# Moving a token mix to GpSimd and cutting three small products into narrow tiles, in a two-block transformer kernel on one core

## The reference, cut to what matters

```python
x_prev = jnp.pad(x, ((0, 0), (1, 0), (0, 0)))[:, :T]
xx = x_prev - x
xs = x[None] + xx[None] * mu[:, None, None, :]      # six mixes
r, k, v = (products of xs[0], xs[1], xs[2] with w_rkv)
w_log = -softplus(-(w0 + tanh(xw @ w1) @ w2)) - 0.5  # xw, xa, xg = xs[3], xs[4], xs[5]
a = sigmoid(a0 + (xa @ a1) @ a2)
g = sigmoid(xg @ g1) @ g2                            # g1 is 1024 x 160
kk = kk / max(sqrt(sum(kk * kk)), 1e-12)             # k * k_k, per head of 64
S, y = scan over the tokens
y = ((y - mean) * rsqrt(var + LNX_EPS)) * lnx_w + lnx_b   # per head of 64
out = ((y + bonus) * g) @ w_o
```

## Time and profile before

| | |
|---|---|
| Median of 3 executions | 1356.43 us (1354.27 to 1356.81) |
| The profiled execution: its time, its span | 1354.54 us, 1352.8 us |
| PE busy | 1318.0 us (97%) |
| DVE busy | 934.7 us (69%) |
| ACT busy | 654.6 us (48%) |
| POOL busy | 96.2 us (7%) |
| Granted TensorE clock, mean | 1.000 |

### The profile page before, as it was taken

The page is one execution under the profiler, slowest core; times in us unless marked ns, Lnnn a source line. Parts: engine busy times, 40 slices in busy tenths (PEclk is TensorE's granted clock), DMA queues, the critical chain, the costliest instruction groups (busy, mean ns, idle before and its releaser), DMA issues.

```text
span 1352.8 us, 23308 instructions
## 1 busy us (share of the span) xinstructions
PE 1318.0 (97%) x9276; PEld 1134.2 (84%) x9276; DVE 934.7 (69%) x1613; ACT 654.6 (48%) x977; POOL 96.2 (7%) x97
## 2 busy tenths in 40 slices
PE   7999999999999999999999998999999999999999
PEld 5987987888888988888888887888888888888887
DVE  6783356877777775877777588666666796576664
ACT  4431323644445775644444577543334568444441
POOL 0003153000000020000001000000001042000000
PEclk9999999999999999999999999999999999999999
DMA  8531213655553233665551550874531432573610
GB/s 241 215 125 64 66 65 99 226 190 192 192 163 110 70 125 112 219 196 189 186 186 62 187 187 1 311 296 171 202 125 63 165 113 75 205 285 138 243 62 32
DMA packets 111126, 208.10 MB, mean 154 GB/s; under 512 B 3872, under 2 KB 53408, under 8 KB 110528
## 3 DMA queue, kind: packets, MB, share of 16 engines
q1 hardware_dynamic: 111040, 206.88, 44.6%
HBM read 205.82 MB, written 1.05 MB: 153 GB/s over the span
## 4 chain that ended last, share of the span: by engine, by line
PE 85%; DVE 8%; ACT 5%; issue 1%; POOL 0%; DMA 0%; SPq 0%; DVEq 0%; ACTq 0%; POOLq 0%
PE ps L991 21%; PE ps L966 18%; PE ps L877 11%; PE ps L971 10%; PE ps L1060 2%; PE ps L1029 2%; PE ps L1377 2%; PE ps L1163 2%; PE ps L1284 1%; PE ps L942 1%; DVE Al L2514 1%; ACT Ah L1775 1%; PE ps L1420 1%; PE ps L1434 1%; ACT arena L2060 1%
## 5 line engine op out<-in xcount | busy, mean ns | idle before, releaser
L966 PE MATMUL ps<-hTx,Ah 128*128 128x512 f32 x1088 | 270.7, 391 | 0.0
L2521 DVE TENSOR_TENSOR Al<-ringA,Ah 128x2048 fp32r<-128x2048 f32 x76 | 173.8, 2287 | 103.4 <-ACT Ah L1785 103.4
L966 PEld LDWEIGHTS ps<-hTx,Ah 128*128 128x128 f32 x1088 | 199.8, 188 | 38.4
L971 PEld LDWEIGHTS ps<-hTx,Al 128*128 128x128 f32 x1152 | 156.7, 191 | 10.6
L971 PE MATMUL ps<-hTx,Al 128*128 128x256 f32 x1152 | 160.7, 283 | 0.0
L1820 ACT COPY xn<-ps 128x512 f32<-128x512 f32 x72 | 42.3, 587 | 243.6 <-PE ps L971 236.3
L1785 ACT CAST Ah<-ringA 128x2048 fp32r<-128x2048 f32 x76 | 145.8, 1919 | 16.7 <-PE ps L877 13.9
L1794 ACT CAST Bh<-ringB 128x1024 fp32r<-128x1024 f32 (+1 forms) x76 | 107.1, 1409 | 89.5 <-PE ps L991 89.5
L877 PE MATMUL ps<-Ah,hTx 128*128 128x512 f32 (+1 forms) x576 | 136.2, 387 | 1.1 <-ACT hTx L1765 0.9
L991 PE MATMUL ps<-Bh,hidh 128*128 128x512 f32 x432 | 135.0, 392 | 1.6 <-issue 1.1
L991 PE MATMUL ps<-Bl,hidh 128*128 128x512 f32 x432 | 134.3, 390 | 0.0
(11 more groups left out here) (433 smaller groups left out, 2013.4 us busy)
## 6 DMA issues: line engine op xcount, KB each, us to landing
ringA<-in_ffn_w_in SPq DMA_DIRECT2D x44, 1024.0 KB, 7.5
ringA<-in_mlp_w SPq DMA_DIRECT2D x32, 1024.0 KB, 7.5
ringB<-in_mlp_w SPq DMA_DIRECT2D x32, 1024.0 KB, 6.9
ringB<-in_ffn_w_out SPq DMA_DIRECT2D x44, 512.0 KB, 4.3
ringA<-in_diff_w_in SPq DMA_DIRECT2D x12, 1024.0 KB, 6.3
ringA<-in_dsa_w_in SPq DMA_DIRECT2D x8, 1024.0 KB, 6.4
ringA<-in_w_k SPq DMA_DIRECT2D x4, 1024.0 KB, 8.3
ringA<-in_w_r SPq DMA_DIRECT2D x4, 1024.0 KB, 7.2
```

Of the source, the lines that this page charges most:

```text
L966: mm(o.rearrange("p (i t) -> p i t", i=2), w_hi, hTx[:, :, k * T:(k + 1) * T], start=(k == 0), stop=False)
L971: last = mm(o[:, T:2 * T], Al[:, half, k * T + j * P:k * T + j * P + P], hTh[:, k, :], start=False, stop=(k == KT - 1))
L2521: V.tensor_tensor(a_split(w, Al, half), a_half(w, (a_at[w] + par) % 2, half), a_split(w, Ah, half).bitcast(F32), ALU.subtract).then_inc(al ...
```

## The change

Four edits, all in the first mixer:

1. **Mix 1 moves to GpSimd.** Per half, four `tensor_scalar` (`xx * mu`, 128x256) and one `tensor_tensor` (`+ hT`, 128x1024). It waits for `xx_rdy`, which VectorE's `shifted` raises, and raises `xa_rdy`.
2. **Narrow tiles.** The gate's last 32 columns are made chunk by chunk into four column tiles of 32 (32 matmuls of 64 columns for 8 of 256); `key_sums` likewise; `key_factors` becomes 32 products of 32 rows and 64 columns, and the root, clamp and inverse act on 64 columns for 256. The second gate product uses 32 rows at partitions 32c, so g2's last rows are loaded four times, with no clearing. Four dummy products (`keep(4, 7)`) are put behind the first gate product.
3. **Order of the gates.** `gates_wide((0, 1))` behind h1, `gates_narrow((0, 1))` behind h2, both pairs 2 and 3 behind the scan.
4. **Chunk 3's norm by lanes.** VectorE does mean, centring and squares for 256 columns at a time, lane 0 before lane 1; GpSimd scales lane 0 and adds its bonus, VectorE does so for lane 1.

```diff
-                             (g2b_sb[0:GLORA - P, :], d["a_g2"][P:GLORA, :]),
+                             *[(g2b_sb[32 * c:32 * c + 32, :], d["a_g2"][P:GLORA, :]) for c in range(NCK)],
...
                 for k in range(KT):
                     a0 = CON["sel"][0] + 14 - 2 * k
-                    last = mm(ps[:, 0, 0:T], con[:, a0:a0 + P], xnflat[:, k * T:(k + 1) * T],
-                              start=(k == 0), stop=(k == KT - 1))
+                    for j in range(4):
+                        o = k * T + j * CH
+                        last = mm(ps[32 * j:32 * j + 32, 0, 0:CH], con[:, a0:a0 + 32],
+                                  xnflat[:, o:o + CH], start=(k == 0), stop=(k == KT - 1))
...
-                for k in (0, 2, 4, 6, 1, 3, 5, 7):
-                    r = slice(32 * (k // 2), 32 * (k // 2) + 32)
-                    last = mm(ps[:, k // 2, (k % 2) * T:(k % 2) * T + T],
-                              spread[r, k * P:(k + 1) * P], kinv[r, :], start=True, stop=True)
+                for k in range(KT):
+                    for j in range(4):
+                        r = slice(32 * j, 32 * j + 32)
+                        last = mm(ps[:, j, k * CH:k * CH + CH], spread[r, k * P:(k + 1) * P],
+                                  kinv[r, :], start=True, stop=True)
...
+            for k in range(KT):
+                o = k * wl + 2 * LORA + P
+                for c in range(NCK):
+                    last = mm(ps[32 * c:32 * c + 32, b, T:T + CH], ringA[:, a % 2, o:o + 32],
+                              xi[:, k, c * CH:c * CH + CH], start=(k == 0), stop=(k == KT - 1))
             last.then_inc(job_rdy, 1)
+            keep(4, 7)
...
+            def gate_part(c, i, left, right, first):
+                return mm(ps[head_rows(i), c, :], left,
+                          right.rearrange("p (k i n) -> p k i n", k=KT, i=2)[:, :, i, :],
+                          start=first, stop=not first)
...
                 if (u, name) == (7, "h1"):
-                    gates(0)
+                    gates_wide((0, 1))
                 elif (u, name) == (7, "h2"):
-                    gates(1)
+                    gates_narrow((0, 1))
...
+            i, buf = MIXES[1]
+            for half in range(2):
+                pool.wait_ge(xx_rdy, half + 1)
+                ks = slice(4 * half, 4 * half + 4)
+                for k in range(4 * half, 4 * half + 4):
+                    last = G.tensor_scalar(fm(buf)[:, k, :], fm(xx)[:, k, :], col("mu", 8 * i + k), None,
+                                           ALU.mult)
+                link(last)
+                G.tensor_tensor(fm(buf)[:, ks, :], fm(buf)[:, ks, :], hT[:, ks, :], ALU.add
+                                ).then_inc(xa_rdy, 1)
...
+            pool.wait_ge(wk["rstd"], 4)
+            link(G.tensor_tensor(groups(y), groups(y), bc(g, 2, 64), ALU.mult))
+            link(G.tensor_tensor(y, y, row("lnx_w")[:, 0:256], ALU.mult))
+            G.tensor_tensor(y, y, bv3[:, 0:256], ALU.add).then_inc(wk["yn"], 1)
...
             shifted(0, 4)
             mix(0, 0)
-            mix(1, 0)
             dve.wait_ge(ha_rdy, 4)
             shifted(4, 8)
             mix(0, 1)
-            mix(1, 1)
...
+            for l in range(2):
+                y, d3, g, _r = last_lane(l)
+                dve.wait_ge(*EV_N[6 + l, "Y"])
+                link(V.tensor_reduce(g, groups(y), AX_X, ALU.add))
+                link(V.tensor_scalar(g, g, 1.0 / HD, None, ALU.mult))
+                link(V.tensor_tensor(groups(y), groups(y), bc(g, 2, 64), ALU.subtract))
+                link(V.tensor_tensor(d3, y, y, ALU.mult))
+                V.tensor_reduce(g, groups(d3), AX_X, ALU.add).then_inc(ss_rdy, 1)
```

More of the change, by code:

```diff
@@ L211, in program @@
         xs_rdy = sem("xs_rdy")
+        xa_rdy = sem("xa_rdy")
+        xx_rdy = sem("xx_rdy")
         wk = {n: sem("wk_" + n) for n in
@@ L1136, in _ @@
                     if k % 4 == 0:
[L1137 removed]
+                        pe.wait_ge((xs_rdy, xa_rdy)[i], k // 4 + 1)
                     o = k * wl + i * LORA
@@ L1143, in _ @@
             xi = fm(MIXES[2][1])
[L1144 to L1150, removed]
+            for k in range(KT):
+                if k % 4 == 0:
+                    pe.wait_ge(xs_rdy, 3 + k // 4)
+                o = k * wl + 2 * LORA
+                mm(ps[:, b, 0:T], ringA[:, a % 2, o:o + P], xi[:, k, :],
+                   start=(k == 0), stop=(k == KT - 1))
+            for k in range(KT):
+                o = k * wl + 2 * LORA + P
+                for c in range(NCK):
+                    last = mm(ps[32 * c:32 * c + 32, b, T:T + CH], ringA[:, a % 2, o:o + 32],
+                              xi[:, k, c * CH:c * CH + CH], start=(k == 0), stop=(k == KT - 1))
             last.then_inc(job_rdy, 1)
+            keep(4, 7)
             for s in range(4):
@@ L1208, in need, with gates_wide, gates_narrow @@
                 pe.wait_ge(*EV_N[u, name])
-            def gates(c):
-                for s, w in ((0, g2a_sb), (T, g2b_sb)):
-                    for i in range(2):
[L1214 to L1219, removed]
+            def gate_part(c, i, left, right, first):
+                return mm(ps[head_rows(i), c, :], left,
+                          right.rearrange("p (k i n) -> p k i n", k=KT, i=2)[:, :, i, :],
+                          start=first, stop=not first)
+            def gates_wide(cs):
+                for c in cs:
+                    for i in range(2):
+                        gate_part(c, i, sigg[:, c * CH:c * CH + CH], g2a_sb, True)
+            def gates_narrow(cs):
+                for i in range(2):
+                    for c in cs:
+                        r = slice(32 * c, 32 * c + 32)
+                        last = gate_part(c, i, sigg[r, T:T + CH], g2b_sb[r], False)
+                        if i:
+                            last.then_inc(wk["g"], 1)
             for u, name in ORDER:
@@ L1313, in _ @@
                 if (u, name) == (7, "h1"):
-                    gates(0)
+                    gates_wide((0, 1))
                 elif (u, name) == (7, "h2"):
-                    gates(1)
[L1318 to L1321, removed]
+                    gates_narrow((0, 1))
+            need(6, "Y")
+            gates_wide((2, 3))
+            gates_narrow((2, 3))
             need(7, "Y")
@@ L2004, in _ @@
                     gn_root(2)
-            gn_root(3)
+            for i, name in enumerate(("lnxc3a", "lnxc3b")):
+                root(name, gs_[:, 56 + 4 * i:60 + 4 * i], gs_[:, 24 + 4 * i:28 + 4 * i], HD, eps_l)
             act.wait_ge(wk["g"], NCK)
@@ L2305, in rest_slot @@
                                 ).then_inc(al_rdy, 1)
[L2307 to L2314, removed]
+            pool.wait_ge(cols_in, 16)
+            i, buf = MIXES[1]
[8 more added lines that the diff above has]
+                                ).then_inc(xa_rdy, 1)
             pool.wait_ge(con_in, 16)
@@ L2889, in _, with last_lane @@
                 gate(c)
[L2890 to L2899, removed]
-            for c in (2, 3):
-                gate(c)
+            def last_lane(l):
+                return (chunk(ytok, 3)[:, 256 * l:256 * l + 256], dl[:, 256 * l:256 * l + 256],
+                        gs_[:, 24 + 4 * l:28 + 4 * l], gs_[:, 56 + 4 * l:60 + 4 * l])
+            for l in range(2):
[6 more added lines that the diff above has]
+                V.tensor_reduce(g, groups(d3), AX_X, ALU.add).then_inc(ss_rdy, 1)
+            dve.wait_ge(sd_rdy, SD["lnxc3a"] + 1)
+            V.reciprocal(last_lane(0)[2], last_lane(0)[3]).then_inc(wk["rstd"], 1)
+            gate(2)
+            y, _d, g, r = last_lane(1)
+            dve.wait_ge(sd_rdy, SD["lnxc3b"] + 1)
+            link(V.reciprocal(g, r))
+            link(V.tensor_tensor(groups(y), groups(y), bc(g, 2, 64), ALU.mult))
+            link(V.tensor_tensor(y, y, row("lnx_w")[:, 256:512], ALU.mult))
+            dve.wait_ge(wk["bv"], 1)
+            link(V.tensor_tensor(y, y, bv3[:, 256:512], ALU.add))
+            gate(3)
             rest_slot(a_at["wo0"], 0)
```

35 lines of the change are left out of this document (19 added, 16 removed).

## The result

The changed kernel takes **1361.8 us** (median of 5, 1360.28 to 1363.65) against 1356.06 (median of 5) for the kernel before, measured beside it: ratio 1.0047, 95% interval 1.0035 to 1.0058. The forecast of 1356.9 and its range up to 1361.0 both missed it, on the slow side. The profiled executions have spans of 1359.4 and 1352.8 us, 6.6 apart.

What follows compares the result with a forecast made beforehand. TensorE, busy 97% of the span, was taken as the bound, with VectorE's mixes leading the chain at the start. 2.1 - 2.35 + 0.8 - 0.1 = +0.45 us gave 1356.9 us on the median, range 1351.2 to 1361.0.

Steps and rivals of the forecast that it cites:

- its `tensor_scalar` ... 256 elements make about 0.34 + 0.19 = 0.55 us: Mix 1 on GpSimd: price of each of its eight multiplies, from a one-element `tensor_scalar` and a copy's slope.
- bounds for the start: Start, mix 1 moved: -0.3 without collision, +1.1 if only the adds collide, +5.8 if GpSimd's whole durations collide.
- sign of being wrong: Start: prediction wrong if VectorE runs through at 0.41 us an instruction or GpSimd's `tensor_scalar` takes far from 0.55 us.
- +2.1: Start: VectorE reaches the key operand 2.1 us later, and TensorE, ready at 34.6, waits for it until 35.5.
- VectorE and GpSimd hold each other off: Start: the two serialize; a half's multiplies cost VectorE 0.44 us and its add 2.2, 5.3 for two halves, less 3.26.
- TensorE falls to its lower clock: Rival, chance 0.08: idle twice for over 2 us, TensorE's clock falls before 30 us; +3, 1359.4 us.
- GpSimd starved: Rival, chance 0.04: GpSimd gets in only at VectorE's waits, the key product starts near 51 us; total about 1372.
- no collision: Rival, chance 0.15: GpSimd reads beside VectorE unharmed; -4.65 us, total 1351.8.
- the tiles don't run together: Rival, chance 0.06: narrow products save nothing; +3.2 us, total 1359.6.
- Key sums and key factors: Narrow key products on TensorE: sums 3.45 to 1.1 us, -2.35; factors 1.08 to 1.9 us, +0.8.
- Gates and chunk 3: Scan's end: narrow gates 0.95 us, Y 0.9 sooner, last tokens turned at 215.1; -0.1, bounds -3.1 and +0.6.
- Behind 216 us nothing is changed, and that work only moves: Everything after 216 us: assumed unchanged, merely shifted in time.

Runs made afterwards that it cites:

- experiment 3: Kernel before plus four more GpSimd multiplies, 128x256 by a column's scalar, ahead of its first copies, where VectorE does nothing yet; 0.92 us each in one profile.
- Experiment 4: Changed kernel with four of GpSimd's eight mix multiplies left out, those blocks filled with zeros ahead of time; 1357.51 us, ratio 1.0015 to the kernel before.
- Experiment 10: Kernel before with only the key sums and key factors made as narrow tiles; 1353.79 us, ratio 0.999.
- Experiment 7: Changed kernel with four filler matmuls on TensorE ahead of its wait for chunk 3's tokens; 1360.36 us, ratio 1.0034 to the kernel before.
- experiment 1: Changed kernel with mix 1 back on VectorE, all else as changed; 1356.7 us, ratio 1.0009 to the kernel before.
- experiment 6: Changed kernel with chunk 3's norm made as a whole on VectorE, as before; 1361.4 us, ratio 1.0039 to the kernel before.
- experiment 11: Changed kernel with all mixes and chunk 3's whole norm back on VectorE, keeping narrow keys, gates and the filler; 1356.53 us, ratio 1.0008 to the kernel before.
- 8: Changed kernel without its own filler of four matmuls ahead of the key product; 1360.75 us, ratio 1.0037 to the kernel before.
- 9: Changed kernel with TensorE filler ahead of both waits for GpSimd's mix and ahead of chunk 3's tokens; 1359.38 us, ratio 1.003 to the kernel before.
- 12: Kernel before with narrow key sums and key factors and four filler matmuls ahead of the wait for chunk 3's tokens; 1356.06 us, ratio 1.0003.

## Why the prediction was wrong

**The start is where it failed, in the term "its `tensor_scalar` ... 256 elements make about 0.34 + 0.19 = 0.55 us".** It is 1.03 us, and 0.92 without company (experiment 3). The prediction took the slope from a copy and the base from a one-element `tensor_scalar`, 0.19 + 0.34. It gave no upper bound for this price at all; with the add's slope of 2.1 ns an element it would have been 0.34 + 0.54 = 0.88 us, and the mix's end 25.2 + 8 x 0.33 = 27.8. Its bounds for the start (-0.3 to +5.8) were made from collisions alone. It named this price as a sign of being wrong, and that sign came true. Experiment 4 shows it from the other side: with four multiplies fewer 4.3 of the 6.4 us go.

**The second step that failed is the clock, which the sum put at nothing.** By the spans the change cost 6.6 us for a forecast of 0.45. Of the 6.15 us between, 2.7 are the late mix (3.56 less the 0.9 of slack below), 1.65 the clock at the start, 1.65 the clock at 220 us, and some 0.2 lie outside the marks. A correct price alone would not have mended the sum: in experiment 4 the mix is on time, the clock falls at both places, and the kernel is 1.6 us above the sum.

**From +2.1 to +6.35 at the start, term by term.** The mix's second half comes 3.56 us late. Of this 3.0 are the multiply's own price, 8 x (0.92 - 0.55), and 0.6 its collisions with VectorE beyond the 1.1 that the forecast had for them. The 14 instructions take 1.45 more and the gate's wide part 0.2 more than priced. The prediction had TensorE ready 0.9 before VectorE, which this lateness uses up first. 3.56 + 1.65 - 0.9 = 4.3, which is the difference of 4.25.

**That VectorE and GpSimd hold each other off was right, and nearly in size.** Each add held one mix instruction off by 2.1 us (2.57 and 2.56 for 0.48), where the prediction had 2.2. What it left out is that `shifted` holds a multiply off in turn, by 0.8. VectorE's 24 remaining mix instructions and what lies between end at 31.76 us for 28.96 with 32 before: +2.8 for a forecast of +2.1. But the chain doesn't run there. The end of the key operand is no longer decided by VectorE, but by ScalarE, whose rounding comes behind the lora job.

**The rival "TensorE falls to its lower clock" (0.08) came true beside the mispriced multiply**, not in its place: it supplies 1.65 us of the start's 6.35. It was priced at +3 for a fall before 30 us, and the fall came there. Experiment 4 shows that it would have come with the price right too (3.06 us for the 14 instructions), and experiment 3 that it can come with the mixes on VectorE. It is in the profiles of all six kernels that have GpSimd's mix and no filler ahead of it, so a chance of 0.08 was far too low. The Trainium skill's rule, TensorE: Matmul & The Clock Gate, section "What's actually happening", that idleness lowers the clock, is now borne out by rows of the changed kernel (0.71 at 24 to 32 us, behind idle spells of 4.50 and 2.90 us); the prediction could show it only at a kernel's start. "GpSimd starved", "no collision" and "the tiles don't run together" did not happen.

**Key sums and key factors were right:** -2.42 and +0.86 for -2.35 and +0.8. The Trainium skill's floor of some 25 ns between starts (same page, "Wait — 56ns, not 53.3ns?") would have made the sums 1.6 us; 64 instructions in 1.03 us are 16 ns apart, so the measurement decides against it for four column tiles. Experiment 10 shows the gain reaches the end.

**Gates and chunk 3, forecast -0.1, came out at 0.0 up to the last turned token and at +1.6 behind it.** The narrow gate product is 1.02 us (forecast 0.95), and from lane 0's copy of Y to the last turned token it is 10.9 us (209.17 to 220.07; forecast 215.1 - 203.8 = 11.3). But the copy comes only 0.4 sooner and not 0.9, against the scan's first step. The two misses cancel, so that this term fits by luck. What was missed above all is that the wait of 1.49 us becomes two of 0.49 and 1.86 us, and that the clock can fall behind them: 0.57 at 220 us. "Behind 216 us nothing is changed, and that work only moves" does not hold: that work ran 1.6 us longer. Experiment 7 removes the fall and about that much between the same marks. The prediction looked for a fall only at the start.

**Not settled:** whether the transfer that reaches into the idle spell at 145 us is what makes it 2.2 us in the two kernels with filler at the start, and why one spell is followed by a fall and its like is not. Which spell costs the kernel before its clock in the executions where the mean is under 1.0 is known for one close relative only: experiment 3, ahead of 23.67 us. It was not tried to give GpSimd only one half of the mix.

## What to carry to other kernels

Price an operation by a row of the same operation with the same kinds of operands; where the trace has only another one, put the dearest neighbour into the bounds, since a base from one row plus a slope from another can be off by two. An engine off the bound may be given work only with slack counted up to the moment its consumer asks, and here TensorE asked after 8 us (22.7) for work that takes GpSimd 14. After any edit that shortens or starves TensorE, list its idle spells: behind any of them the clock may fall, anywhere in the kernel. Here it fell behind spells from 0.94 to 4.5 us, not behind each of them, and a fall lengthened the work behind it by 1.3 to 3.0 us. A filler helps only inside a wait.

## What the runs showed of the hardware

- GpSimd's multiply by a column's scalar, 128x256 fp32: 0.92 us with VectorE idle, 1.03 beside VectorE's mixes, 1.84 beside its `shifted`; a copy of 128x512 0.61.
- A GpSimd add (both inputs in SBUF, 128x1024, 2.35 us) kept one VectorE mix instruction, 0.48 us alone, at 2.57 and 2.56 us. GpSimd's multiplies did not: three mixes took 1.48 us beside them.
- Of two nearly equal idle spells, 1.86 us in the changed kernel and 1.85 in experiment 1, each behind one of 0.5, the first was followed by a fall of the clock and the second was not. The same holds for 2.85 us in experiment 6 (fall, 0.50 at 218 to 220) and 2.87 us in experiment 11 (none). So one profile doesn't tell how often a kernel pays.
- The time of an execution goes with its mean granted clock, in the kernel before too: of the 24 executions beside experiments 4, 8, 9 and 12, 10 with 1.0 had a median of 1354.8 us, 10 with 0.999 1356.1, and 4 with 0.997 1357.0. The changed kernel's five had 0.994 to 0.996.
- Four column tiles of 32 weight columns and 64 moved ones run together: 64 instructions in 1.03 us.
